# Work moved at seven stage edges of a two-group streaming encoder step

## What is computed

```python
def run_trunk(x, ...):                         # DEPTH = 2, D_MODEL = 1024, D_FF = 2816
    for i in range(DEPTH):
        x = x + 0.5 * swiglu(rmsnorm(x, norm_g[i, 0]), ffn_w_gu[i, 0], ffn_w_d[i, 0])
        xn = rmsnorm(x, norm_g[i, 1])
        if i % 2 == 0:
            y, st = even_mixer(xn, ...)        # gated DeltaNet heads and mLSTM heads, then @ w_out
        else:
            y, st = odd_mixer(xn, ...)         # gated short convolution, then @ w_out
        x = x + y
        x = x + 0.5 * swiglu(rmsnorm(x, norm_g[i, 2]), ffn_w_gu[i, 1], ffn_w_d[i, 1])
        xg = rmsnorm(x, norm_g[i, 3])
        x = x + (p[i] @ w_ple[i]) * jax.nn.sigmoid(xg @ w_ple_gate[i])
    return rmsnorm(x, final_norm), st_even..., st_odd
```

## Time and profile before

| | us |
|---|---|
| median of 3 runs | 2746.33 |
| lowest and highest | 2745.28, 2747.19 |
| the profiled execution's own time | 2744.97 |
| its span, first to last instruction | 2743.2 |
| TensorE (PE) busy | 2655.2 (97%) |
| VectorE (DVE) busy | 1867.2 (68%) |
| ScalarE (ACT) busy | 1079.1 (39%) |
| POOL busy | 521.1 (19%) |
| DMA: bytes, mean rate | 205.57 MB, 75 GB/s |

### The profile page before, as it was taken

How to read it: one execution, slowest core, us unless ns; L and a number is a source line. 1 busy time by engine, 2 the same in 40 slices (tenths; PEclk the granted TensorE clock), 3 DMA queues, 4 the chain that set the end, 5 groups by cost and what they waited for, 6 DMA issues and landing times.

```text
span 2743.2 us, 43569 instructions
## 1 busy us (share of the span) xinstructions
PE 2655.2 (97%) x18131; PEld 2617.2 (95%) x18131; DVE 1867.2 (68%) x2183; ACT 1079.1 (39%) x1576; POOL 521.1 (19%) x247
## 2 busy tenths in 40 slices
PE   6999999999999999999999899999999999999997
PEld 6999999999998799999999899999999999999997
DVE  7848476988667778476576884847666786574755
ACT  5525244233222645344344452524411254352444
POOL 3020303232010030301113202030333311102031
PEclk9999999999999999999999999999999999999998
DMA  3323323232003222223222232332222223232321
GB/s 105 90 70 88 92 73 82 55 87 55 16 9 72 75 71 78 85 77 93 72 79 68 70 88 69 91 92 71 85 78 78 62 77 93 71 92 70 91 81 47
DMA packets 401244, 205.57 MB, mean 75 GB/s; under 512 B 15650, under 2 KB 399035, under 8 KB 401048
## 3 DMA queue, kind: packets, MB, share of 16 engines
q1 hardware_dynamic: 400842, 202.70, 26.0%
q10 hardware_dynamic: 206, 0.08, 0.0%
HBM read 195.14 MB, written 7.60 MB: 74 GB/s over the span
## 4 chain that ended last, share of the span: by engine, by line
PE 56%; DVE 8%; ACT 1%; issue 1%; POOL 0%; DVEq 0%; ACTq 0%
PE ps L881 9%; PE ps L896 9%; PE ps L898 9%; PE ps L897 9%; PE ps L885 9%; PE ps L882 9%; DVE ut L1997 1%; DVE r L2105 1%; DVE hf L2500 1%; DVE x L2775 0%; DVE sumsq L2093 0%; DVE x L2591 0%; DVE wlo L2013 0%; PE ps L1112 0%; DVE hl L2082 0%
## 5 line engine op out<-in xcount | busy, mean ns | idle before, releaser
L833 POOL TENSOR_TENSOR wlo<-raw,whi 128x1024 fp32r<-128x1024 f32 (+2 forms) x210 | 509.8, 2431 | 2176.6 <-ACT whi L1514 2176.6
L881 PE MATMUL ps<-xh,whi 128*128 128x320 f32 x1488 | 456.4, 314 | 21.8 <-POOL wlo L833 5.6
L882 PE MATMUL ps<-xl,whi 128*128 128x320 f32 x1488 | 451.5, 311 | 0.0
L881 PE MATMUL ps<-hh,whi 128*128 128x320 f32 x1440 | 438.3, 312 | 12.6 <-DVE hl L2082 4.4
L882 PE MATMUL ps<-hl,whi 128*128 128x320 f32 x1440 | 435.3, 310 | 0.0
L896 PE MATMUL ps<-tau_hi,whi 128*128 128x320 f32 x1328 | 411.2, 310 | 4.9 <-ACT sq L1661 2.8
L897 PE MATMUL ps<-tau_lo,whi 128*128 128x320 f32 x1328 | 410.4, 309 | 0.0
L898 PE MATMUL ps<-tau_hi,wlo 128*128 128x320 f32 x1328 | 410.3, 309 | 0.0
L1514 ACT CAST whi<-raw 128x1024 fp32r<-128x1024 f32 (+2 forms) x210 | 202.1, 963 | 394.7 <-PE ps L885 352.7
L885 PE MATMUL ps<-xh,wlo 128*128 128x320 f32 x1488 | 341.6, 311 | 0.0
L885 PE MATMUL ps<-hh,wlo 128*128 128x320 f32 x1440 | 329.5, 310 | 0.0
(11 more groups left out here) (405 smaller groups left out, 4919.6 us busy)
## 6 DMA issues: line engine op xcount, KB each, us to landing
raw<-in_ffn_w_gu SPq DMA_DIRECT2D x332, 256.0 KB, 3.9
raw<-in_ffn_w_d SPq DMA_DIRECT2D x64, 512.0 KB, 4.0
raw<-in_w_in_even SPq DMA_DIRECT2D x32, 512.0 KB, 4.1
raw<-in_ffn_w_d SPq DMA_DIRECT2D x32, 384.0 KB, 3.5
raw<-in_w_in_odd SPq DMA_DIRECT2D x24, 512.0 KB, 3.7
raw<-in_w_ple_gate SPq DMA_DIRECT2D x16, 512.0 KB, 3.9
raw<-in_ffn_w_gu SPq DMA_DIRECT2D x10, 512.0 KB, 3.9
raw<-in_w_out_even SPq DMA_DIRECT2D x8, 512.0 KB, 4.1
```

Of the source, the lines that this page charges most:

```text
L833: pool.tensor_tensor(ring(wlo, n), raw[:, slot, 0:kt, :], ring(whi, n).bitcast(fp32), ALU.subtract).then_inc(lo_ready, 1)
L881: pe.matmul(ps[j % 4][:, c, 0:HT], wh[:, k], hi[:, k, cs], start=(k == 0), stop=False)
L882: pe.matmul(ps[j % 4][:, c, 0:HT], wh[:, k], lo[:, k, cs], start=False, stop=False)
```

## The change

1. **Opening.** The first SwiGLU has three plain pairs instead of two. The norm job still follows the first up block. ScalarE's and VectorE's lists are written for it: the root comes before the last two rounds of token sums, and VectorE makes the fourth token sum (`tau_sums_alone(3)`) after the first gate is scaled instead of at the start.
2. **Sample tile's start.** ScalarE's copy of the last tile's output (`o_kept`) moves behind the exponentials; VectorE's update of the mLSTM state (`mlstm_part(t - 1, "up1")`) moves ahead of its wait for them.
3. **Sample tile's end.** TensorE makes the spreads of heads 4 to 7 in a row, ahead of the halves of `w_out`'s first two blocks. VectorE adds the last state and normalises head 4 before it makes head 3's low part.
4. **Gate weights.** In both last `down` stages before a `ple` stage, ScalarE casts the block after next (`w_ple_gate`'s first in layer 0, `w_ple`'s third in layer 1) before the square of x's last piece, instead of at the start of `ple`.
5. **The end of layer 0's `ple`.** ScalarE makes the high part of the last two pieces before their squares, and casts the third round of token sums before the last piece. VectorE updates x's seventh piece before it makes the sums and low parts of the sixth.
6. **Layer 1's first SwiGLU** has two plain pairs instead of one, with lists of its own (`plain_twice`).
7. With two more blocks in them, two runs of blocks get other pieces of the ring: the opening's, and the one from layer 0's last `down` stage to layer 1's first pair, whose second block takes pieces 3 and 4 instead of 5 and 6.

The diff, cut to its core (the two new lists of the opening and of `plain_twice` whole):

```diff
-                s["plain"] = 0 if part else 2 if prod == 1 else 1
+                s["plain"] = 0 if part else 3 if prod == 1 else 2 if i == 1 and f == 0 else 1
...
-                o_spread(4)
+                for q in range(HA, 2 * HA):
+                    o_spread(q)
...
                 mm(n, hi, lo, first=(h_ready, s["hbase"]), part=(0, HA))
-                o_spread(5)
...
-                o_spread(6)
...
                 mm(n + 1, hi, lo, part=(0, HA))
-                o_spread(7)
...
-                        if s["plain"] == 1:
+                        if s["plain"] < 3:
                             norm_job(s)
...
# ScalarE
-                    if s["plain"] == 2:
+                    if s["plain"] == 3:
                         prep(s["g0"] + 2)
                         tau_round(s["tau"], 0)
                         tau_round(s["tau"], 1)
                         prep(s["g0"] + 3)
+                        norm_root(s)
+                        prep(s["g0"] + 4)
+                        gate(0)
                         tau_round(s["tau"], 2)
+                        high(0)
+                        prep(s["g0"] + 5)
+                        gate(1)
+                        tau_round(s["tau"], 3)
+                        prep_pair(p0, 0)
+                        high(1)
+                        prep_pair(p0, 1)
+                        gate(2)
+                        prep_pair(p0, 2)
+                        prep_pair(p0, 3)
+                    elif s["plain"] == 2:
+                        prep(s["g0"] + 2)
+                        tau_round(s["tau"], KH - 1)
                         norm_root(s)
-                        tau_round(s["tau"], 3)
+                        prep(s["g0"] + 3)
                         gate(0)
...
                         prep_next(s["n0"] + o, 2)
+                        if "pT" in s and o == KD - 1:
+                            prep_next(s["n0"] + KD, 2)
...
-                    act.copy(qkv[:, 16:16 + HA, (t - 1) * P:t * P], heads(2)).then_inc(o_kept, 1)
...
                     act.activation(kcol[:, 4:8], gcols[:, GC - HA:GC], ACT.Exp).then_inc(core["eg"], 1)
+                    act.copy(qkv[:, 16:16 + HA, (t - 1) * P:t * P], heads(2)).then_inc(o_kept, 1)
...
-                        produce(s["next"], o, s["g"] if s["i"] + 1 < DEPTH else None, last=o == KD - 1)
+                        produce(s["next"], o, s["g"] if s["i"] + 1 < DEPTH else None, last=o >= KD - 2)
...
-                    prep_next(s["n0"], 2)
...
+                        if s["tau"] is not None and open_gate == KD - 1:
+                            tau_round(s["tau"], KH - 2)
...
# VectorE
                 mul(v, v, heads(0))
+                mlstm_part(t - 1, "up1")
...
-                mlstm_part(t - 1, "up1")
...
+                add_s(3)
+                normalise(4)
                 low(3)
-                add_s(3)
-                for q_ in range(HA, 2 * HA):
+                for q_ in range(HA + 1, 2 * HA):
...
+                    def plain_twice():
+                        tau_rest(s["tau"], KH - 1)
+                        norm_recip(s)
+                        plain_gate(0)
+                        first = sums_13(p0)
+                        sums_2(p0, first)
+                        plain_hidden(0)
+                        hidden_low(0)
+                        plain_gate(1)
+                        pair_low(p0, 0)
+                        sums_4(p0)
+                        pair_low(p0, 1)
...
+                        if g is not None and o == KD - 2:
+                            produce(s["next"], KD - 3, g)
+                            tau_step(KD - 3)
+                            x_low(s["next"], KD - 2, g)
                     if g is not None:
-                        x_low(s["next"], KD - 2, g)
+                        tau_step(KD - 2)
                         x_low(s["next"], KD - 1, g)
```

More of the change, by code:

```diff
@@ L1677, in _ @@
                         prep(s["g0"] + 3)
+                        norm_root(s)
+                        prep(s["g0"] + 4)
+                        gate(0)
                         tau_round(s["tau"], 2)
+                        high(0)
[11 more added lines that the diff above has]
+                        tau_round(s["tau"], KH - 1)
                         norm_root(s)
-                        tau_round(s["tau"], 3)
+                        prep(s["g0"] + 3)
                         gate(0)
+                        high(0)
                         prep_pair(p0, 0)
-                        high(0)
+                        gate(1)
                         prep_pair(p0, 1)
-                        gate(1)
                         prep_pair(p0, 2)
@@ L1940, in finish @@
                     def finish(o):
-                        produce(s["next"], o, s["g"] if s["i"] + 1 < DEPTH else None, last=o == KD - 1)
+                        produce(s["next"], o, s["g"] if s["i"] + 1 < DEPTH else None, last=o >= KD - 2)
                         if s["tau"] is not None and o % 2 == 0:
                             x_back(s["tau"], o, s["g"])
-                            if o:
+                            if 0 < o < KD - 2:
                                 tau_round(s["tau"], o // 2 - 1)
@@ L2532, in plain_start @@
                         t = s["tau"]
-                        tau_sums_alone(3)
                         tau_rest(t, 0)
@@ L2537, in plain_start @@
                         plain_gate(0)
+                        tau_sums_alone(3)
+                        plain_hidden(0)
+                        plain_gate(1)
+                        tau_rest(t, 2)
+                        hidden_low(0)
                         first = sums_13(p0)
                         sums_2(p0, first)
-                        tau_rest(t, 2)
+                        tau_rest(t, 3)
+                        plain_hidden(1)
                         pair_low(p0, 0)
-                        tau_rest(t, 3)
+                        hidden_low(1)
+                        sums_4(p0)
+                        plain_gate(2)
+                        pair_low(p0, 1)
[5 more added lines that the diff above has]
+                        sums_2(p0, first)
                         plain_hidden(0)
+                        hidden_low(0)
+                        plain_gate(1)
+                        pair_low(p0, 0)
+                        sums_4(p0)
                         pair_low(p0, 1)
-                        hidden_low(0)
-                        sums_4(p0)
-                        plain_gate(1)
-                    if s["plain"] == 2:
+                    if s["plain"] == 3:
                         plain_start()
+                    elif s["plain"] == 2:
+                        plain_twice()
                     elif s["plain"]:
@@ L2767, in _ @@
                         free(j)
-                        if 0 < o < KD - 1:
+                        if 0 < o < (KD - 1 if g is None else KD - 2):
                             produce(s["next"], o - 1, g)
                             tau_step(o - 1)
+                        if g is not None and o == KD - 1:
+                            square_sum(s["next"], KD - 2)
                         dve.wait_ge(act_out, s["act0"] + o + 1)
@@ L2775, in _ @@
                         own(dve.tensor_tensor(x[:, o, :], x[:, o, :], ut[:], ALU.add).then_inc(x_new, 1), x_new)
+                        if g is not None and o == KD - 2:
+                            produce(s["next"], KD - 3, g)
+                            tau_step(KD - 3)
+                            x_low(s["next"], KD - 2, g)
                     if g is not None:
-                        x_low(s["next"], KD - 2, g)
+                        tau_step(KD - 2)
                         x_low(s["next"], KD - 1, g)
-                    square_sum(s["next"], KD - 2)
-                    square_sum(s["next"], KD - 1)
-                    tau_step(KD - 2)
-                    tau_step(KD - 1)
+                        square_sum(s["next"], KD - 1)
+                        tau_step(KD - 1)
+                    else:
+                        square_sum(s["next"], KD - 2)
+                        square_sum(s["next"], KD - 1)
                 elif kind == "odd_in":
```

## The result

| | before | changed |
|---|---|---|
| median of 5 runs, us | 2747.19 | 2730.23 |
| lowest and highest | 2745.28, 2750.99 | 2729.75, 2735.61 |
| ratio, 95% interval | | 0.9945 (0.9934 to 0.9956) |
| the profiled execution's own time | 2744.97 | 2733.02 |

The account below looks back on a forecast made before the run. TensorE, busy 97% of the span, was taken as the bound, so only its idle or slow-clock time pays. Terms sum to 23.8 us off 2744.97: 2721.2, or 2722.5 against the median; range 2716.5 to 2731.0.

Parts of the forecast that it names:

- What bounds the kernel, and the price of a wait: Whole kernel: TensorE busy 97%; a long wait also costs 1.5 to 2.9 us of slower matmuls behind it.
- Opening: First SwiGLU: wait before up block 1 shrinks to 2.5 us, clock stays up, copy's wait goes; 5.6 us gained.
- the lower case I had named: Opening: only 2.5 us gained if the clock still falls and the copy still waits 1.5.
- Sample tile's start: Copy of 0.59 us leaves ScalarE's chain ahead of TensorE's wait near 870; 0.5 us gained, between -0.5 and 1.
- Core's end: Spreads 4 to 7 in a row ahead of the half blocks; 5.1 us gained, 2.9 of it clock.
- rival 3: Core's end: VectorE is the bound, head 4 not ready before 970; 2727.6 us, chance 0.10.
- Ring and start of `ple`: Layer 0: last `down` block's pieces free earlier, 0.7 us; gate block cast earlier, at full clock, 4.0 us gained.
- Rival 2: Both `ple` stages: casts stay where they were because the ring holds them; 2729.5 us, chance 0.08.
- End of `ple`: Into layer 1's first SwiGLU: x first only moves the wait, plain blocks replace slow pair; 4.9 us gained.
- rival 4: Opening and layer 1's first SwiGLU: plain pairs only pay for themselves, a cast is waited for; 2733.0 us, chance 0.10.
- Layer 1's `ple`: Start of the stage: earlier cast puts the second block in time, no lower clock behind it; 3.0 us gained.

Follow-up runs that it names:

- e3: The kernel before with only the opening's three plain pairs; median 2739.89 us against 2746.25 before.
- e6: The changed kernel without the edits at the sample tile's start and the core's end; median 2728.47 us against 2746.25 before.
- e13: The changed kernel with spreads 4 to 7 split two and two and without the sample tile's start edit; median 2725.18 us against 2744.84 before.
- e14: The changed kernel with spreads two and two and 24 overwritten matmuls in the wait for x's eighth low part; median 2723.74 us against 2744.84 before.
- e9: The changed kernel with spreads 4 and 5 ahead of the first half block, 6 and 7 before the second; median 2724.34 us against 2744.99 before.
- e4: The changed kernel without the sample tile's start edit; median 2729.11 us against 2745.13 before.
- e8: The changed kernel timed again, unaltered; median 2729.88 us against 2745.13 before.

## Why the prediction was wrong

- **What bounds the kernel, and the price of a wait:** right. A drop after a wait costs 1.5 (26.42 or 27.98 for the same work).
- **Opening:** right in size and chain; POOL's hold on both rests is in the trace. That the clock stayed up was in part luck: in four of the twelve traces with this opening (e3, e6, e13, e14) it did fall, at about 53, and the term was 3.9 to 4.2, against 5.5 to 6.1 in the other eight. That is the lower case I had named, without the 1.5 for the copy.
- **Sample tile's start:** right in size, 0.44 to 0.55, but no more than executions differ by there: the stretch took 9.0 to 9.5 in the ten traces with part 2 and 9.1 to 10.4 in the seven without, 0.6 apart on average. Whether the moved work changes the clock behind it is not settled: in the ten traces with part 2 the tile took 76.0 on average, in the seven without 74.0, but the medians of e13 and e9, e4 and e8 differ by 1 or less, in both directions.
- **Core's end:** the step that failed. It said that the rest "ends at 976.15", with every matmul at 0.1467 us. I had just charged the old waits with a lower clock, and then let a stage with three waits left (0.49, 0.92, 0.82) and 48 small matmuls ahead of the first half block run at 1.00. The chain of waits is right: no wait for `hl` remained, and rival 3 did not happen. The term was mis-sized by the clock: 1.3 to 2.0 instead of 5.1. The bank's wait was priced at 0.5 and is 0.92 in three of the eight traces and 0 to 0.50 in five; what I had put at nothing is that four spreads in a row bring the clock down, with or without that wait. Four spreads in a row at full clock would take about 26.5 (an estimate: 29.6 less the 3 or so that the drop cost, 1.3 on the spread and 1.8 on the half block), which is the 31.6 - 5.1 forecast; they never got it.
- **Ring and start of `ple`:** right, 4.64 of 4.7, with the order at the shared port the other way than assumed. Rival 2 did not happen.
- **End of `ple`:** 4.0 to 4.7 of 4.9 (3.5 to 5.0 over the seven traces with this code), for the wrong reason. "Putting x ahead of the token sums moves the wait and buys nothing" was wrong: a wait one step later has one step less behind it. The second plain pair, to which the term was charged, came near to what rival 4 says of it, that it only pays for itself, though no cast is waited for.
- **Layer 1's `ple`:** 2.91 of 3.0, and half of it luck. The trace of before has a drop of the clock there (1.5 of the term) that three of the six traces with that code lack; against those three the edit brings 1.35.
- **What was missing from the range:** the tile. I took the time of a stretch that the change hardly touches from one execution. It was up to 7.5 us longer in another, and the range's upper end (2731.0 against 2746.33, or 0.9944) left no room for that beside a failed term. Measured, 0.9945.

## What to carry to other kernels

Price a wait with the slow matmuls behind it, and ask the same of the waits that the change leaves or makes: a stage of small matmuls with several short waits may run at the lower clock in either order. Spread the small matmuls between large ones rather than collecting them; here that brought 2.5 to 3.7 us of one stretch. Where a wait of some us can't be removed, matmuls whose result is overwritten can keep the clock up, and cost nothing if they end before it; here they shortened the stretch in two of two traces, and no median showed it.

Cut two traces at the same instruction and compare stretches that the edit does not touch; their difference is the error of the method, here up to 7.5 us in one stretch.

## What the runs showed of the hardware

- The same instructions, with the same code ahead of them, meet a different number of stretches at half clock from one execution to the next: the tile took 80.7 and 77.5 us in two traces of one kernel (73.1 to 80.7 over all 17), and layer 1's `ple` 26.4 or 28.0 with the same code there. The Trainium skill ("TensorE: Matmul & The Clock Gate", section "Part 1: The HAM clock gate") says as much of the start of a kernel, that the number of slow matmuls varies between runs of one kernel; here it holds in its middle.
- In all 15 traces with the wait of 4.1 to 4.4 for x's seventh or eighth piece the clock fell in its last 2 us or within 1.1 us behind it; with fillers in it, in two of two, it did not. After the wait of 1.8 in layer 1's `ple` it fell in three of six.
- Of the spreads (12 matmuls of 24 rows, 1.5 us each), one ahead of the large matmuls left the clock up in five of five traces; with two it fell right behind them in three of four, with four among them in eight of eight, in five of these before any of them had waited for a bank.
- A VectorE operation of two SBUF operands that started 0.45 us after one of POOL ended 0.68 after it, 1.8 us later than alone (2.63 instead of 0.83), and two in a row behind two of POOL took 5.79 instead of 3.02.
